# The first attention's maxima scaled on GpSimd, partition maxima replaced by TensorE's sums, and steps of the norm between two blocks moved

## The reference

```python
x = rms_norm(x, final_g)                      # end of the first block
h = _rms(x, a_norm)                           # start of the second
q, k, v, g = split(h @ w_in)                  # 8 heads, q and k in two sides of 64
qs = [rope(_rms(q[..., c, :], q_norm)) for c in range(2)]      # ks likewise
a = softmax(mask(q1 k1 * scale)) - lam * softmax(mask(q2 k2 * scale))
o = _rms(a @ v, subln) * (1 - lambda_init)
x = x + (o * silu(g)) @ w_out
```

## Time and profile before

| | us |
|---|---|
| median of three executions | 2531.79 |
| lowest, highest | 2530.01, 2536.81 |
| the profiled execution | 2530.41 |
| its span in the trace | 2528.6 |

### The profile page before, as it was taken

The page is one execution under the profiler, slowest core; times in us unless marked ns, Lnnn a source line. Parts: engine busy times, 40 slices in busy tenths (PEclk is TensorE's granted clock), DMA queues, the critical chain, the costliest instruction groups (busy, mean ns, idle before and its releaser), DMA issues.

```text
span 2528.6 us, 30214 instructions
## 1 busy us (share of the span) xinstructions
PE 2363.5 (93%) x12840; PEld 1252.4 (50%) x12840; DVE 1519.4 (60%) x1962; ACT 968.2 (38%) x1383; POOL 216.0 (9%) x263
## 2 busy tenths in 40 slices
PE   6999999999999999898999777899999998888899
PEld 4445444444444444344444455654444445666764
DVE  6898755644454455777631488965534307888862
ACT  5245334212121212323321466732323116777741
POOL 0001030000000002324201101022000000000000
PEclk9999999999999999898999899999999998999999
DMA  4010011110101010121011000021130100000021
GB/s 177 34 67 34 1 34 63 70 67 34 67 34 67 34 67 34 36 101 67 34 67 34 1 1 1 8 93 34 67 133 34 68 1 34 1 1 1 1 84 50
DMA packets 50326, 116.00 MB, mean 46 GB/s; under 512 B 2386, under 2 KB 7819, under 8 KB 49808
## 3 DMA queue, kind: packets, MB, share of 16 engines
q1 hardware_dynamic: 48456, 105.40, 11.8%
q10 hardware_dynamic: 1736, 8.68, 0.8%
HBM read 101.49 MB, written 12.58 MB: 45 GB/s over the span
## 4 chain that ended last, share of the span: by engine, by line
PE 76%; DVE 13%; ACT 6%; issue 3%; DMA 1%; POOL 1%; ACTq 0%; DVEq 0%; POOLq 0%
PE PS L72 72%; ACT RG L81 4%; PE PS L75 3%; DVE R L93 2%; DVE R L101 2%; DVE RG L107 2%; DVE mx L110 2%; DVE RG L101 2%; ACT OV L84 1%; DVE scl L110 1%; DMA RG<-in_a_w_in 1%; DVE RG L93 1%; DVE oss L110 1%; ACT R L81 1%; ACT OV L81 0%
## 5 line engine op out<-in xcount | busy, mean ns | idle before, releaser
L72 PE MATMUL PS<-R,RG 128*128 128x512 f16 (+1 forms) x5472 | 1167.6, 375 | 10.2 <-DVE RG L101 4.7
L72 PEld LDWEIGHTS PS<-R,RG 128*128 128x128 f16 (+1 forms) x5472 | 543.4, 103 | 631.8 <-issue 14.5
L72 PE MATMUL PS<-RG,R 128*128 128x512 f16 x2880 | 634.6, 381 | 4.5 <-DVE R L101 4.0
L72 PEld LDWEIGHTS PS<-RG,R 128*128 128x128 f16 x2880 | 282.7, 98 | 337.8 <-issue 7.5
L81 ACT ACTIVATE R<-PS,scl 128x512 f32<-128x512 f32 (+1 forms) x192 | 126.8, 687 | 716.1 <-PE PS L72 616.3
L101 DVE SCALAR_TENSOR_TENSOR R<-PS,scl,R 128x512 f32<-128x512 f32 (+1 forms) x208 | 148.7, 746 | 149.2 <-PE PS L72 124.1
L107 DVE TENSOR_TENSOR_SCAN RG<-RG 128x127 f32<-128x127 f32 (+7 forms) x128 | 168.6, 1345 | 110.4 <-ACT RG L81 110.1
L72 PE MATMUL PS<-R,OV 128*128 128x64 f32 (+2 forms) x1456 | 194.5, 286 | 34.9 <-DVE R L93 32.8
L101 DVE SCALAR_TENSOR_TENSOR RG<-RG,scl 128x4096 f16<-128x4096 f32 (+1 forms) x43 | 188.7, 4389 | 52.2 <-ACT RG L81 52.2
L72 PEld LDWEIGHTS PS<-R,OV 128*128 128x128 f32 x1456 | 180.6, 199 | 45.1 <-DVE R L93 39.3
L75 PE MATMUL PS<-ident,RG 128*128 128x128 f32 x864 | 148.5, 289 | 47.1 <-ACT OV L84 23.9
(11 more groups left out here) (120 smaller groups left out, 1546.7 us busy)
## 6 DMA issues: line engine op xcount, KB each, us to landing
RG<-in_w_ff SPq DMA_DIRECT2D x16, 2048.0 KB, 8.1
RG<-in_a_w_in SPq DMA_DIRECT2D x8, 2048.0 KB, 8.5
RG<-in_w_in SPq DMA_DIRECT2D x4, 2048.0 KB, 9.6
xspill<-R ACTq DMA_DIRECT2D x2, 4096.0 KB, 15.3
RG<-in_w_kv SPq DMA_DIRECT2D x4, 2048.0 KB, 8.0
RG<-in_b_w_in SPq DMA_DIRECT2D x4, 2048.0 KB, 7.9
R<-in_x SPq DMA_DIRECT2D x8, 512.0 KB, 9.1
RG<-in_w_out SPq DMA_DIRECT2D x2, 2048.0 KB, 7.7
```

The lines of the kernel that those rows point to most:

```text
L72: return self.engine.matmul(*a, **k) if self.engine else Nothing()
```

## The change

- `BOUNDED`: for the tiles 24, 25, 26, 27 and 30 GpSimd's all-reduce goes. TensorE multiplies the column of partition peaks by ones (`bound`), which gives in every partition their sum, an upper bound of the maximum, and DVE makes the factor from it. For 24 to 27 `bound` stands ahead of the q/k product at which the tile is to be converted, for 30 ahead of the gate products of t = 2.
- The times of tiles 23 to 28 are set anew: 23 is converted at (21, 13); 24 measured at (22, 6) and converted at (23, 5); 25 (24, 2) and (24, 4); 26 (24, 7) and (25, 1); 27 (25, 4) and (25, 6); 28 (26, 2) and (26, 4).
- The norm between the blocks: `spread("final_g", 0)` and `final_x(0)` leave the feed-forward part for q/k (TensorE at u = 6, DVE at u = 7 and 8); the second half's sums go from u = 1 to 2, its spreads from 2 and 6 to 3 and 10, `final_h(1)` from two units to four, `final_x(1)` to u = 10 and 11, the spill to u = 12.
- The last gate tile's peak and their maximum go from before the attention to group 3, tile 31's peak in four quarters to groups 8 to 11. Both peaks' sums over the partitions are made by TensorE in group `da_first` + 6 (`tops`, bank 6) and copied by DVE one group later.
- The 86 scalings of the row maxima go from DVE (`top`) to GpSimd (`scale_top`). GpSimd's `finish_tile` is cut into halves; those of i = 0 to 3 stand between the scalings of groups 30 to 37, those of i = 7 behind the last scaling.

```diff
-for _i in (7, 8, 19, 20, 21, 22, 23, 30, 31, 32, 33, 35):
+for _i in (7, 8, 19, 20, 21, 22, 23, 24, 25, 26, 30, 31, 32, 33, 35):
     del MEASURE[_i, 1], CONVERT[_i, 2]
...
-                   (21, (19, 1), (19, 2)), (22, (19, 6), (20, 1)), (23, (20, 7), (21, 9)),
-                   (24, (23, 2), (23, 3)), (25, (22, 7), (23, 5)), (32, (30, 7), (30, 8)),
+                   (21, (19, 1), (19, 2)), (22, (19, 6), (20, 1)), (23, (20, 7), (21, 13)),
+                   (24, (22, 6), (23, 5)), (25, (24, 2), (24, 4)), (26, (24, 7), (25, 1)),
+                   (27, (25, 4), (25, 6)), (28, (26, 2), (26, 4)), (32, (30, 7), (30, 8)),
...
+BOUNDED = (24, 25, 26, 27, 30)
...
+            def bound(i):
+                b = banks.take(("bound", i))
+                e.wait_ge(*sig("w_peak").at(i))
+                e.wait_ge(*banks.free(("bound", i)))
+                e.matmul(b[:, 0:1], ones[:, :], w_col(i, 0), start=True, stop=True).then_inc(*full.up("bound", i))
+            def feed(i, use):
+                if CONVERT.get((i, use)) in BOUNDED:
+                    bound(CONVERT[i, use])
...
-                if j == 12:
-                    spread("final_g", 0)
...
-                if u == 1:
+                if u == 2:
                     sums("final", 1)
-                if u == 2:
+                if u == 3:
                     spread("a_norm_2", 1)
-                if u == 6:
-                    spread("final_g", 1)
+                if u in (6, 10):
+                    spread("final_g", u // 10)
+                feed(22 + 2 * which + c, t + 1)
                 product_n(22 + 2 * which + c, t, ("qk", u), ready=h_ready("a_norm_2", t // 4))
...
+                if u == da_first + 6:
+                    b = banks.take_at(("tops",), 6)
+                    e.wait_ge(*sig("o_peak").at())
+                    e.wait_ge(*sig("w_peak").at(31))
+                    e.wait_ge(*banks.free(("tops",)))
+                    e.matmul(b[:, 0:1], ones[:, :], col(123), start=True, stop=True)
+                    for j in range(4):
+                        mm = e.matmul(b[:, 1:2], ones[:, :], tile31_peak(j), start=(j == 0), stop=(j == 3))
+                    mm.then_inc(*full.up("tops"))
...
-                if j == 11:
-                    diagonal(("a_norm_2", 0), ("final_g", 0), 0)
-                if j in (12, 13):
-                    final_x(0, range(4 * j - 48, 4 * j - 44))
                 down(key, j % 8 + 9)
...
-                e.tensor_reduce(out, z, AX.X, ALU.max, negate=True).then_inc(*step.up())
-                e.wait_ge(*step.last())
-                e.tensor_scalar(m, m, ssc, None, ALU.mult).then_inc(*sig("top_a").up(u, sides[-1]))
+                e.tensor_reduce(out, z, AX.X, ALU.max, negate=True).then_inc(*sig("peak_a").up(u, sides[-1]))
...
+                if u == 3:
+                    gate_peak(NT - 1)
+                    e.wait_ge(*step.last())
+                    e.tensor_reduce(col(123), col(32, 8), AX.X, ALU.max).then_inc(*sig("o_peak").up())
+                if 8 <= u < 12:
+                    j = u - 8
+                    e.wait_ge(*sig("raw").at(31))
+                    up_ = sig("w_peak").up(31) if j == 3 else step.up()
+                    e.tensor_reduce(tile31_peak(j), w_raw(31)[:, 1024 * j:1024 * j + 1024], AX.X, ALU.max,
+                                    apply_absolute_value=True).then_inc(*up_)
...
+                if u == da_first + 7:
+                    e.wait_ge(*full.at("tops"))
+                    e.tensor_copy(col(126, 2), banks.ap(("tops",))[:, 0:2]).then_inc(
+                        *banks.empty([("tops",)], sig("bank_dve"), "tops"))
...
-                if u == 9:
+                if u == 12:
                     spill()
...
             def measure(i):
+                if i in BOUNDED:
+                    return
                 e.wait_ge(*sig("w_peak").at(i))
                 across(w_col(i, 1), w_col(i, 0)).then_inc(*sig("w_top").up(i))
...
+            def scale_top(u, sides):
+                m = da_scale(u, sides[0])
+                m = mx[:, m:m + len(sides) * len(da_groups[u][1])]
+                e.wait_ge(*sig("peak_a").at(u, sides[-1]))
+                e.tensor_scalar(m, m, ssc, None, ALU.mult).then_inc(*sig("top_a").up(u, sides[-1]))
+            for u in range(N):
+                if u < da_first:
+                    scale_top(u, (0, 1))
+                else:
+                    scale_top(u, (0,))
+                    scale_top(u, (1,))
+                if 8 <= u - da_first < 16:
+                    finish_tile((u - da_first - 8) // 2, u % 2)
+            finish_tile(7, 0)
+            finish_tile(7, 1)
```

## The result

| | before | after |
|---|---|---|
| median, us | 2530.93 (20 executions) | 2541.86 (20 executions) |
| lowest, highest | 2527.37, 2538.3 | 2537.32, 2553.51 |
| span of the profiled execution | 2528.6 | 2539.3 |

The ratio after to before is 1.0048, with a 95% interval of 1.0037 to 1.0059: the change makes the kernel slower by 9 to 15 us. The forecast was no change, 2531 us. The same kernel, run once more beside three of the experiments, gave 1.0060 (1.0039 to 1.0081).

A forecast was written before the change was run, and what follows sets the result against it. TensorE was taken to bound the kernel, holding 76% of the chain, so time counts only where it waits or runs at lower clock. The terms summed to -0.6 us on the 2531.79 median: 2531 us, range 2518 to 2542.

The forecast's parts named there:

- Term 1: End of the feed-forward part: TensorE's 12.27 us wait for a diagonal goes; -12.3 us (-9 to -14).
- Term 2: q/k products: TensorE's waits for GpSimd's rotations and the lower clock behind them go, with spill moved and all-reduces gone; -15.7 us.
- Term 3: q/k products: TensorE's sums wait for DVE's tile peaks, then run at lower clock; +22.4 us (14 to 27).
- Term 4: Start of the attention: first exp 6.0 us sooner, perhaps 0.5 of slow clock; moved peak reduces cost +5.9 us later.
- Term 5: Attention, row-maximum scalings on GpSimd: -0.7 us in groups with i < 4, +1.5 us with i >= 4.
- Term 6: Attention, tops and finish: TensorE's transposes wait for bank 6, +2.8 us; `finish_tile` halves hold joins, +2.0; together +4.8 (0 to 8).
- The moved `final_x`, h steps and diagonals [...]: nothing.: q/k units 2 to 11: the moved steps fit into DVE's spare time and cost nothing.
- A wait of 0 to 1.5 us.: q/k, u = 2: TensorE's sums of the second half wait for GpSimd's adds of squares; 1.5 us taken.
- The slower one, by the port: Attention: DVE's join shuts GpSimd's scaling of side 1 out of SBUF, 13 us, 2544 us; chance 2 in 10.
- The faster rival: q/k products: TensorE's new waits for peaks stay short, 2517 us, with none 2509; chance 3.3 in 10.
- The change does not do what it says: q/k: rotations wait even without spill and all-reduce, half the saving stays away, 2539 us; counted as slower, no own chance.

## Why the prediction was wrong

The measured 2541.9 us lie just inside the end of the range, 2542, but that is luck: this end was set by rivals that did not come true, and the forecast of no change is missed. Forecast and trace, term by term (us):

| term | forecast | in the trace |
|---|---|---|
| 1. end of the feed-forward part | -12.3 | +2.1 |
| 2. waits in q/k go | -15.7 | -16.8 |
| 3. TensorE's bounds | +22.4 | +22.5 |
| 4. attention starts sooner | -6.5 | -5.6 |
| 4. the reduces come back, and 5. scaling, i < 4 | +5.2 | +5.1 |
| 5. scaling, i >= 4 | +1.5 | +3.7 |
| 6. tops | +2.8 | +2.0 |
| 6. halves of `finish_tile` | +2.0 | +0.5 |
| sum | -0.6 | +13.5 |

Measured terms: 1 is the gap at u = 10 less that at the start; 2 the steps at the three waits, 8.8 and 2.3 at u = 15 and 16, 2.3 + 1.7 and 1.8 at u = 21 and 29; 3 is 14.2 of waits, 1.7 + 2.35 + 2.5 of clock and 1.8 of small matmuls with the gaps around them; the scalings are 0.12 us for each of some 30 groups (0.95 over the eight of i = 6), the tops what i = 4 grew beyond 8 x 0.12. With the 0.6 at the start and 0.1 in the v and gate products it makes the 14.3 of the last exp within rounding.

**Term 1 failed, by 14.4 us, and with it the forecast.** Two of its steps:
- "The moved `final_x`, h steps and diagonals [...]: nothing." The cost that I looked for was DVE's time, and that is nothing indeed. What I did not follow is a resource that a moved step holds. Spread over four units, the h steps keep the spread's PSUM bank until 1086.4; the banks go round by eights, and between that spread (the fifth take of q/k) and product u = 6 (the thirteenth) lie eight takes. In the kernel before the steps were done three units sooner, and the eighth take behind that spread was the second spread of `final_g`, not a product. 6.35 us of wait and 1.5 of clock; the experiment with two units gave 9 back.
- "A wait of 0 to 1.5 us." I had the low half in the way of GpSimd, but let its last add end at 1044 to 1047.5; it ended at 1050.16. The low half came at 1035.50, not 1033. It held GpSimd's add of 1036.07 for 5.05 us, and DVE's last residuals too, so that the last squares come only from 1040.7 on; seven adds of 1.3 us stand in a row behind the held one. Then the clock: 1.7 on the sums and 2.55 on the product, for which this place had no term although terms 3 and 6 had one. 8.3 us for the 1.5.

**Term 2 had the right size, but not the whole reason.** The gap behind an all-reduce was on the path of all three waits, as the earlier trace rows had it, but at each of them it took a second delay to make TensorE wait: the late load at tile 25, the low half beside the rotation at 26 and 27. Taken away alone, these second delays took the waits with them, all-reduces and gaps kept. So the all-reduces did not have to go, and term 3 was a price paid for nothing (the two experiments with all-reduces kept). None of the 86 scalings in the attention shows such a gap. The Trainium skill's GPSIMD Engine Reference (Instruction dispatch) has the gap, of some 6 us, at the first call of a freshly loaded kernel. The traces agree in the size, 5.65 us ahead of an all-reduce and 7.40 behind it in the run that had them back; the gaps stand at every change between all-reduces and ordinary operations of the q/k products, and that a kernel is loaded there is not shown.

**Term 3 was right**, waits of 1.99, 6.05 and 6.16 for the 2.3, 6.4 and 6.4 forecast. The rows of a clean unit and of one tile's steps were enough for it; the bounds' distance from the peaks is the whole cost, and the experiment took it away by moving them.

**Term 4 right**, both halves within 1 us, the second taken together with term 5's -0.7, from which the trace does not separate it; the wait for the silu in bank 0 is there too (1.45 us).

**Term 5 mis-sized for i >= 4**, +3.7 for +1.5. A scaling of one element takes GpSimd 0.28 to 0.31 us, not the 0.16 that I extrapolated from 307 and 453 ns at 64 and 128 columns: the line through two sizes does not go on below 64, the time stays near that of 64 elements (which was another operation, `TENSOR_TENSOR`). From the end of the reduce to exp it is 0.40, inside the 0.26 to 0.47 given, but not near the end that I chose; 0.12 to 0.13 more in each group.

**Term 6 right in its sum of signs**, the tops 2.0, the halves less than thought: each does hold its join (1.85 us for the 1.02 of a join of i = 5 with nothing beside it), but the join is not on the chain there.

**The rivals.** The slower one, by the port, is refuted: the scaling of side 1 starts 0.09 us behind its reduce (1528.19 behind 1526.54 + 1.56), ahead of the join (1528.46), and takes 0.31.

```profile
1528.19 0.31 POOL L96 TENSOR_SCALAR mx<-mx,scl 128x1 f32<-128x1 f32 x1 [0.45 <-DVE mx L110]
...
1528.46 0.89 DVE L101 SCALAR_TENSOR_TENSOR RG<-RG,oss 128x640 f32<-128x640 f32 x1
```

Where GpSimd does read SBUF beside a join, the join is drawn out: 1.85 us with a half of `finish_tile`, 1.02 without (in the kernel before). The Trainium skill's SBUF — State Buffer (Who interferes with whom) also says that issue order decides who blocks. The traces agree: the scaling, which starts first, keeps its 0.31 us, and the rotation's step of 1178.62 above, which starts behind the low half, is held to 4.51; the halves of `finish_tile` decide nothing, since they start within 0.01 us of their joins. The faster rival is refuted by the waits. The time came out near the 2539 of "The change does not do what it says", but not by that way: TensorE waited for no rotation, and nothing of term 2 stayed.

## What to carry over

When a step is moved or stretched, follow not only its engine's time but what it holds while it is not finished: count the PSUM takes from the one it holds to the one that gets the same bank. A chain of small steps over several in-order engines (peak, factor, convert, low half) can be made cheap by the times at which they stand rather than by a faster engine for one of them: the tile times alone, moved later and three units apart, gave 13 us in the kernel before (part of it by taking a load out of the way of the spill), the change with all its parts gave none. When a single write goes to a PSUM bank that others need in every group, try emptying it by the first instruction of the next group: as its last it cost 4.7 us in the trace here.

## What was not expected of the hardware

- GpSimd's one-element `TENSOR_SCALAR` takes 0.28 to 0.31 us (0.294 in the mean of 64), DVE's 0.214, and the way from DVE to GpSimd and on to ACT adds 0.08 and 0.03.
- The lower clock behind a wait of 2 us cost one product 1.7 us in every trace where there was one; behind 5.6 to 6.4 us it was 1.3 to 2.9 in different executions of one sequence (6.69 to 8.27 for 5.34).
- The second attention, the same work in all kernels here, took from 320.3 to 336.8 us from its first to its last exp in the profiled executions, at a mean granted clock of 0.94 (320 us) to 0.88 (337 us). A comparison of spans of single executions is uncertain by that. The stretches between landmarks in the part that was changed vary less, but they vary too: from the spread of `a_norm_2` to the last gate silu the changed kernel took 410.7 us in one trace and 407.1 in its second.
